# Forget-gate products pass by pass, and three strips of the first modulation tile summed by TensorE

## The reference

```python
silu_c = jax.nn.silu(c)
mod = silu_c @ ada_w[l] + ada_b[l]                    # 1024 -> 3072
shift, scale, gate = jnp.split(mod[:, None, :], 3, axis=-1)
h = rms_norm(h_res, norm_pre_w[l]) * (1.0 + scale) + shift
z = h @ w_in[l]                                        # 1024 -> 6144
u_pool, g_pool, q, f_pre, i_in, g_h = jnp.split(z, ...)
...
f = lb + (1.0 - lb) * jax.nn.sigmoid(f_pre)            # the forget gate
```

## Time and profile before

| | us |
|---|---|
| median of 3 runs | 1116.25 |
| lowest, highest | 1116.17, 1116.38 |
| the profiled execution's own time | 1116.9 |
| its span in the profile | 1115.0 |
| TensorE busy (matmul) | 1102.2 |
| TensorE weight loads, beside the matmuls | 932.6 |
| VectorE busy | 743.6 |
| ScalarE busy | 507.4 |
| GpSimd busy | 19.8 |

### The profile page before, as it was taken

How to read it: one execution, slowest core, us unless ns; L and a number is a source line. 1 busy time by engine, 2 the same in 40 slices (tenths; PEclk the granted TensorE clock), 3 DMA queues, 4 the chain that set the end, 5 groups by cost and what they waited for, 6 DMA issues and landing times. The chain is left out here.

```text
span 1115.0 us, 18068 instructions
## 1 busy us (share of the span) xinstructions
PE 1102.2 (99%) x7344; PEld 932.6 (84%) x7344; DVE 743.6 (67%) x1195; ACT 507.4 (46%) x851; POOL 19.8 (2%) x40
## 2 busy tenths in 40 slices
PE   8999999999999999999999999999999999999997
PEld 7888888888888888878888787887788999999986
DVE  6866766954676247448789896446558777667753
ACT  7562354334675225533352434336543444443543
POOL 1000000000001001000000000000000000000000
PEclk9999999999999999999999999999999999999999
DMA  9643324332214423522223232131111322333241
GB/s 372 220 145 112 119 84 132 124 96 78 76 57 150 154 90 108 191 70 82 77 76 95 76 95 75 58 113 58 58 61 72 114 72 99 115 114 113 73 193 75
DMA packets 33618, 121.09 MB, mean 109 GB/s; under 512 B 3824, under 2 KB 3824, under 8 KB 33536
## 3 DMA queue, kind: packets, MB, share of 16 engines
q1 hardware_dynamic: 30672, 109.88, 29.2%
q0 software_dynamic: 2720, 10.03, 2.6%
q10 hardware_dynamic: 144, 0.03, 0.0%
HBM read 115.74 MB, written 4.19 MB: 108 GB/s over the span
## 5 line engine op out<-in xcount | busy, mean ns | idle before, releaser
L1160 DVE TENSOR_TENSOR w_lo<-raw,w_hi 128x1024 fp32r<-128x1024 f32 (+2 forms) x194 | 225.8, 1165 | 151.9 <-ACT w_hi L649 148.9
L1825 PE MATMUL acc<-hT_hi,w_hi 128*128 128x512 f32 x680 | 271.9, 400 | 0.4 <-DVE hT_lo L1143 0.4
L1827 PE MATMUL acc<-hT_hi,w_lo 128*128 128x512 f32 x680 | 265.6, 391 | 0.0
L1826 PE MATMUL acc<-hT_lo,w_hi 128*128 128x512 f32 x680 | 265.2, 390 | 0.0
L649 ACT ACTIVATE w_hi<-raw 128x1024 fp32r<-128x1024 f32 (+2 forms) x194 | 195.2, 1008 | 111.5 <-PE acc L1827 85.6
L1825 PEld LDWEIGHTS acc<-hT_hi,w_hi 128*128 128x128 f32 x680 | 128.0, 188 | 28.9 <-issue 3.7
L1827 PEld LDWEIGHTS acc<-hT_hi,w_lo 128*128 128x128 f32 x680 | 127.7, 188 | 27.3
L1826 PEld LDWEIGHTS acc<-hT_lo,w_hi 128*128 128x128 f32 x680 | 128.0, 188 | 24.8
L1825 PE MATMUL acc<-w_hi,hT_hi 128*128 128x512 f32 (+1 forms) x152 | 60.3, 397 | 0.0
L1827 PE MATMUL acc<-w_hi,hT_lo 128*128 128x512 f32 (+1 forms) x152 | 58.8, 387 | 0.0
L1826 PE MATMUL acc<-w_lo,hT_hi 128*128 128x512 f32 (+1 forms) x152 | 58.8, 387 | 0.0
(11 more groups left out here) (455 smaller groups left out, 2217.1 us busy)
## 6 DMA issues: line engine op xcount, KB each, us to landing
raw<-in_ga SPq DMA_DIRECT2D x32, 512.0 KB, 4.6
ada_raw<-in_ada SPq DMA_DIRECT2D x16, 512.0 KB, 11.1
raw<-in_wo SPq DMA_DIRECT2D x16, 512.0 KB, 3.5
raw<-in_br SPq DMA_DIRECT2D x16, 512.0 KB, 3.6
raw<-in_q SPq DMA_DIRECT2D x8, 512.0 KB, 3.5
raw<-in_u SPq DMA_DIRECT2D x8, 512.0 KB, 4.3
raw<-in_gp SPq DMA_DIRECT2D x8, 512.0 KB, 4.6
raw<-in_ada_w SPq DMA_DIRECT2D x8, 512.0 KB, 3.5
```

Source lines behind the costliest of these rows:

```text
L1160: nc.vector.tensor_tensor(out=lo[:, 0:width], in0=strip_of(k), in1=hi[:, 0:width].bitcast(f32), op=ALU.subtract).then_inc(lo_made, 1)
L1825: nc.tensor.matmul(ps, w[0], x[0], start=first, stop=False)
L1826: nc.tensor.matmul(ps, w[0], x[1], start=False, stop=False)
L1827: return nc.tensor.matmul(ps, w[1], x[0], start=False, stop=last)
```

## The change

The last token tile of x is fetched ahead of the second modulation tile. Strips 5 to 7 of modulation tile 0 are multiplied by TensorE directly, and `sum_mod(0)` moves behind the first turned block of the last x tile. The heads' x copies are made in plain order. fk 0 is written as an interleave of three passes, fk 1 to 7 as three passes in full (all seven high x high products, the modulation sum of the next tile, all seven high x low, all seven low x high), with a separate wait ahead of each pass. ScalarE splits weights ahead of `modulate_h`; VectorE makes the low part of h tile 0 ahead of the low weights. SyncE waits for `mod_summed` also for the slot of modulation tile 1.

```diff
-FETCH = [("x", 0), ("x", 1), ("ada", 0), ("x", 2), ("ada", 1), ("x", 3), ("fk", 0), ("ada", 2), ("ada", 3)]
+FETCH = [("x", 0), ("x", 1), ("ada", 0), ("x", 2), ("x", 3), ("ada", 1), ("fk", 0), ("ada", 2), ("ada", 3)]
...
-BY_PE = {1: [6, 7]}
+BY_PE = {0: [5, 6, 7], 1: [6, 7]}
...
-XT_COPIES = [1, 2, 7, 3, 4, 5, 6]
+XT_COPIES = [1, 2, 3, 4, 5, 6, 7]
...
-                        if last == 3:
-                            sp.wait_ge(mod_summed, 2)
+                        if last in (1, 3):
+                            sp.wait_ge(mod_summed, last // 2 + 1)
...
-                if k + 1 < KT:
-                    modulate_h(k + 1)
                 if (kind, j) not in (("wo", 14), ("wo", 15)):
                     for later_k in to_split(k):
                         split_hi(later_k)
+                if k + 1 < KT:
+                    modulate_h(k + 1)
...
+            lower_h(0)
             split_lo(0)
-            lower_h(0)
...
             for t in range(TT):
-                if t == TT - 1:
-                    sum_mod(0)
                 pe.wait_ge(x_rstd, t + 1)
                 for kt in range(KT - 1):
                     ins = turn_tile(t, kt)
                     if t == TT - 1:
                         ins.then_inc(xT_made if kt else x0_made, 1)
+                        if kt == 0:
+                            sum_mod(0)
...
                 if kind == "fk":
-                    hi, lo = weights(k)
-                    pe.wait_ge(h_lo, j + 1)
-                    for h in range(HEADS - 1):
-                        cols = slice(h * P, (h + 1) * P)
-                        if j == 0:
-                            if h:
-                                pe.wait_ge(xT_copied, XT_COPIES.index(h) + 1)
-                        ins = product((acc + side)[h][:, :], (hi[:, cols], lo[:, cols]), (hT_hi[:, j, :], hT_lo[:, j, :]),
-                                      j == 0, j == KT - 1)
-                        if j == KT - 1 and h < HEADS - 2:
-                            ins.then_inc(f_heads_made, 1)
-                        if h == 2 and j == 0:
-                            pe.wait_ge(xT_copied, XT_COPIES.index(7) + 1)
-                            sum_mod(1)
-                        if h == 4 and j + 2 < KT:
-                            sum_mod(j + 2)
+                    hi, lo = split_at(k)
+                    def head_part(h, w, x, start, stop):
+                        return nc.tensor.matmul((acc + side)[h][:, :], w[:, h * P:(h + 1) * P], x[:, j, :],
+                                                start=start and j == 0, stop=stop and j == KT - 1)
+                    def upper(h):
+                        return head_part(h, hi, hT_hi, True, False)
+                    def lower_x(h):
+                        return head_part(h, hi, hT_lo, False, False)
+                    def lower_w(h):
+                        return head_part(h, lo, hT_hi, False, True)
+                    pe.wait_ge(hi_made, k + 1)
+                    pe.wait_ge(h_hi, j + 1)
+                    if j == 0:
+                        pe.wait_ge(h_full, 1)
+                        for h in range(HEADS - 1):
                             if h:
                                 pe.wait_ge(xT_copied, XT_COPIES.index(h) + 1)
+                            upper(h)
+                            if h >= 1:
+                                pe.wait_ge(h_lo, 1)
+                                lower_x(h - 1)
+                            if h >= 3:
+                                pe.wait_ge(lo_made, 1)
+                                lower_w(h - 3)
+                        lower_x(HEADS - 2)
+                        pe.wait_ge(xT_copied, XT_COPIES.index(7) + 1)
+                        sum_mod(1)
+                        for h in range(HEADS - 4, HEADS - 1):
+                            ins = lower_w(h)
+                    else:
+                        for h in range(HEADS - 1):
+                            upper(h)
+                        if j + 1 < KT:
+                            sum_mod(j + 1)
+                        pe.wait_ge(h_lo, j + 1)
+                        for h in range(HEADS - 1):
+                            lower_x(h)
+                        pe.wait_ge(lo_made, k + 1)
+                        for h in range(HEADS - 1):
+                            ins = lower_w(h)
+                            if j == KT - 1 and h < HEADS - 2:
+                                ins.then_inc(f_heads_made, 1)
                     ins.then_inc(unit_used, 1)
```

## The result

| | before | after |
|---|---|---|
| median, us | 1116.24 (10 runs) | 1119.59 (10 runs) |
| lowest to highest | 1116.15 to 1116.62 | 1117.96 to 1120.96 |
| the profiled execution | 1116.9 | 1118.09 |
| its span | 1115.0 | 1116.2 |

The ratio of the times is 1.0026, with a 95% interval of 1.0019 to 1.0034; from the medians it is 1.0030. The change makes the kernel slower by about 3.3 us, where +1.6 was forecast (range 1116.6 to 1118.7).

A forecast was written before the change was run, and what follows sets the result against it. TensorE's own stream bounds the kernel (busy 1102.2 of 1115.0 us). fk 1 starts 0.5 earlier, fk 6 gains a 0.50 sum, q0 waits 1.4: q0 at 62.45 against 60.85, +1.6, forecast 1117.8 us, range 1116.6 to 1118.7.

The forecast's parts named there:

- Fetch order: Start: x 3 is fetched in ada 1's place, so turning x 3 starts at 13.08 instead of 13.59; gain 0.51 us.
- Tile 0: Modulation tile 0: sum of 16 records behind x 3's first turned block; fk 0 at 17.4 against 16.75, 0.65 lost.
- fk 0 in passes: First forget-gate products, interleaved: no wait inside; TensorE idles 0.8 us after them; fk 1 counts as 24.5, 0.5 earlier.
- fk 1 to 6: Forget-gate blocks: same products, sum of tile j+1, thin VectorE margins but no wait; fk 6 gets one sum, 0.50 us.
- The end of fk: Tile 7's sum runs 3.45 us later against the stream; room is 1.38, so TensorE waits 1.4 for q0's low weights.
- SyncE's wait: Fetch queue: ada 9 also waits for the first modulation sum, issued at about 15.1 instead of 12.3; costs nothing.
- rival C: fk 1 to 7: clock falls to 1.2 GHz, adding 33 us, total 1151; sign a PEclk digit under 9; chance 0.02.
- A: At q0: no wait, the room of 1.38 us is enough; sum 0, 1116.3 us; chance 0.07.
- B: fk 0 to 7: changing banks each product costs; 4 ns each adds 0.6 us, 12 ns gives 1119.9; chance 0.06.
- D: Start slips: tile 0's sum or fk 1's margins fail, fk 1 no earlier than 24.98; 1118.3 to 1119 us; chance 0.05.
- E: Faster: the start gains all of 0.51 and the 1.28, and q0 does not wait; some 1114 us; chance 0.02.

## Why the prediction was wrong

The steps of the sum held. **Fetch order:** x 3 came 0.6 earlier, and ada 1 ended VectorE's sum no earlier. **Tile 0:** fk 0 began 0.5 later than before (0.65 forecast), bound by TensorE's turning; the sixteen records took 14.55 - 12.84 = 1.71, or 0.107 each, as priced. **fk 0 in passes:** no wait inside; fk 1 at 24.6 in the frame of before, against 24.4. **fk 1 to 6:** no wait; the thin margins held and the lag at tile 2 was made up. **The end of fk:** the wait for q0's low weights was 1.2, with restart and latency what was priced; moving the constants took 1.4 off. **SyncE's wait** cost nothing. In the lower group the whole comes to 1118.1 - 1116.2 = 1.9, where 1.6 was forecast; in the profiles q0 lies 62.41 - 60.85 = 1.56 later, and the last 0.3 is not placed.

The step that failed is rival C, the clock. It was given 0.02, on the ground that "the row of the granted clock stays full through the 64 turning records over 8 banks". That row was from a kernel without the new light stretches, and it answered the wrong question: whether changing banks drops the clock. That it doesn't, is right: in the changed kernel's profile fk 6 begins at 50.56 and the last three products of fk 7 at 59.91, so the two take 59.91 - 50.56 + 3 x 0.227 = 10.03 us, which is 42 products at 0.227 and a sum of 0.50, with the clock full. But the prediction itself had put twelve one-column records more on TensorE, priced at 0.105 each, and "TensorE idles 0.8" before fk 1, priced at its length. Each carried a second price: behind each of them the clock can be at half for some 3 us, which costs up to 1.6. In the profiles it was behind tile 0's sum in two kernels and behind the pause in two (one of them the execution at 0.75). This term was missing from the sum: the median run lies 1.5 of its 3.35 us above the lower group.

Rival C also had the size and the sign wrong. It had the clock low through all of fk 1 to 7, for 33 us or 1151 us in all; the falls seen lasted 3.4 us. A 512-column product at half clock cost (26.96 - 25.68) / 3 = 0.43 us there, and not twice 0.227. And its sign, a digit of the clock row under 9, could not have shown what happened: the page of the run with the fall reads 9 throughout. The evidence against C, the same row in the kernel before, was blind to a fall of this length too.

The Trainium skill, "TensorE: Matmul & The Clock Gate", section "A second HAM failure mode: psum-queue depth-cycling", tells of a bf16 kernel in which short idle times between groups of matmuls made the clock go back and forth. The prediction read it as a rule on banks and set it against rows of the turning, whose one idle time in the earlier trace rows is 0.40 us. The traces agree with it in part: the clock fell behind a pause of 0.63 us, but it also fell behind tile 0's sum with no idle time, and it stayed full behind a pause of 1.28 us in the kernel before.

The rivals: A falls (the wait is there), B falls (fk's products keep 0.227), D did not occur, and neither did E. The chances for slower were 0.12 where the interval of the ratio has most of its weight above +0.2%.

What stays open: why the kernel before, with the same twelve records and a longer pause (1.28, but six products in between and none of the sum's records right ahead), was above in only 1 of 111 runs; why both light stretches together gave 20 of 27 runs above and each alone 2 and 3 of 11 (if each fell on its own at these rates, an estimate is four in ten); what it is about the sixteen records; and whether runs 3 us above lose it twice, as their size suggests.

## What to carry to other kernels

Where TensorE runs without a gap, a step that makes it light for a microsecond or two (one-column products, short waits) is to be priced with what the clock may take, not at its own length, and one profile may show none of it: look at the spread of the runs and at the granted clock of each. A pause that can't be removed may be filled with zero products that end before the awaited operand comes; here they cost nothing and took the runs above from 6 of 21 to 0 of 22. Nor does the clock row of a page settle the matter: with slices of 28 us it rounds a fall of 3.4 us away, and windows of 1 us show it. And when a modulation sum is moved later in the stream, follow everything queued behind it on the other engine up to the next step's operands: small work without a due time (the constants here) belongs behind them.

## What was not expected of the hardware

The clock fell behind an idle time of only 0.63 us, and behind tile 0's sum with no idle time in its rows at all (busy 1.00 in the window ahead of the fall): a full row of busy time does not tell what the clock will do. Each fall seen ended by itself after some 3 us, with the products going on. It also begins late: in the changed kernel's run the clock was still full (1.00) through the pause and fell only 0.4 us after the products had started again. The same program showed it in some executions and not in others, on the same chip in one series.
